# Causal attention with the scores once, query rows on partitions, and the probabilities turned by TensorE

## What is computed

```python
qb = jnp.moveaxis(q.reshape(B, nb, ATTN_BLOCK, H, Dq), 1, 0)       # Dq = 64 + 32, ATTN_BLOCK = 128
def one_block(args):
    q_blk, i = args
    s = jnp.einsum('bqhd,bkhd->bhqk', q_blk, k).astype(jnp.float32) * scale
    s = jnp.where(kpos[None, :] <= qpos[:, None], s, -jnp.inf)
    p = jax.nn.softmax(s, axis=-1).astype(v.dtype)
    return jnp.einsum('bhqk,bkhd->bqhd', p, v)                     # values are 64 wide
```

## Time and profile before

| | |
|---|---|
| runs of the kernel before | 1379.83, 1379.10, 1374.12 us, median 1379.10 |
| the profiled execution | 1374.35 us, span 1372.6 us |
| granted TensorE clock, mean | 0.993 |
| TensorE busy | 1327.3 us, 97% |
| VectorE busy | 917.8 us, 67% |
| ScalarE busy | 452.4 us, 33% |
| GpSimd busy | 492.0 us, 36% |

### The profile page before, as it was taken

How to read it: one execution, slowest core, us unless ns; L and a number is a source line. 1 busy time by engine, 2 the same in 40 slices (tenths; PEclk the granted TensorE clock), 3 DMA queues, 4 the chain that set the end, 5 groups by cost and what they waited for, 6 DMA issues and landing times.

```text
span 1372.6 us, 22898 instructions
## 1 busy us (share of the span) xinstructions
PE 1327.3 (97%) x9644; PEld 1075.2 (78%) x9644; DVE 917.8 (67%) x997; ACT 452.4 (33%) x615; POOL 492.0 (36%) x306
## 2 busy tenths in 40 slices
PE   7999999999999989988999999999999999999997
PEld 6877677777776689985678878888888888888886
DVE  4657974363654544436787789877776786669877
ACT  3144543233344333323114431222212444333330
POOL 0000122040577100100065787767664355444030
PEclk9999999999999999999999999999999999999999
DMA  5111354678348942223123235444445986656662
GB/s 221 62 47 46 123 184 154 165 178 255 116 137 279 231 126 55 50 73 138 62 107 108 85 130 177 166 157 154 141 144 202 357 285 229 198 185 194 201 200 110
DMA packets 144726, 213.77 MB, mean 156 GB/s; under 512 B 79368, under 2 KB 82064, under 8 KB 143984
## 3 DMA queue, kind: packets, MB, share of 16 engines
q1 hardware_dynamic: 144336, 211.26, 48.3%
q10 hardware_dynamic: 288, 1.05, 0.2%
HBM read 137.76 MB, written 66.39 MB: 149 GB/s over the span
## 4 chain that ended last, share of the span: by engine, by line
PE 50%; DVE 2%; POOL 1%; issue 1%; ACT 0%; DVEq 0%; POOLq 0%; ACTq 0%
PE banks L2508 22%; PE banks L2398 18%; PE banks L2314 6%; PE banks L2386 2%; POOL tile_h L3064 1%; PE banks L2359 1%; POOL tile_s L3064 0%; PE banks L2340 0%; PE banks L156 0%; DVE first_relu L2856 0%; PE banks L2325 0%; DVE wout_lo L2719 0%; DVE y_all L2739 0%; DVE y_all L2735 0%; PE banks L150 0%
## 5 line engine op out<-in xcount | busy, mean ns | idle before, releaser
L2508 PE MATMUL banks<-stage_b_hi,stage_a_hi 128*128 128x512 f32 x448 | 174.3, 389 | 0.0
L2508 PE MATMUL banks<-stage_b_lo,stage_a_hi 128*128 128x512 f32 x448 | 174.3, 389 | 0.0
L2508 PE MATMUL banks<-stage_b_hi,stage_a_lo 128*128 128x512 f32 x448 | 174.3, 389 | 0.0
L2884 DVE TENSOR_TENSOR stage_a_lo<-stage_a_raw,stage_a_hi 128x1024 fp32r<-128x1024 f32 x56 | 100.6, 1796 | 40.2 <-ACT stage_a_hi L2648 40.2
L2648 ACT ACTIVATE stage_a_hi<-stage_a_raw 128x1024 fp32r<-128x1024 f32 x56 | 59.4, 1061 | 119.6 <-DMA stage_b_raw<-in_w_ffn 99.0
L2508 PEld LDWEIGHTS banks<-stage_b_lo,stage_a_hi 128*128 128x128 f32 x448 | 84.1, 188 | 17.6
L2508 PEld LDWEIGHTS banks<-stage_b_hi,stage_a_lo 128*128 128x128 f32 x448 | 84.1, 188 | 17.5
L2508 PEld LDWEIGHTS banks<-stage_b_hi,stage_a_hi 128*128 128x128 f32 x448 | 84.1, 188 | 17.3
L428 PE MATMUL banks<-xT_hi,win_hi 128*128 128x512 f32 x288 | 90.6, 396 | 0.0
L428 PE MATMUL banks<-xT_lo,win_hi 128*128 128x512 f32 x288 | 88.8, 389 | 0.0
L428 PE MATMUL banks<-xT_hi,win_lo 128*128 128x512 f32 x288 | 88.7, 389 | 0.0
(11 more groups left out here) (424 smaller groups left out, 3585.9 us busy)
## 6 DMA issues: line engine op xcount, KB each, us to landing
stage_b_raw<-in_w_ffn SPq DMA_DIRECT2D x50, 512.0 KB, 5.0
stage_a_raw<-hid_s SPq DMA_DIRECT2D x32, 512.0 KB, 4.0
w_landed<-in_w_ffn SPq DMA_DIRECT2D x30, 512.0 KB, 4.9
hid_s<-tile_s SPq DMA_DIRECT2D x60, 256.0 KB, 4.3
stage_a_raw<-hid_h SPq DMA_DIRECT2D x24, 512.0 KB, 4.1
hid_h<-tile_h SPq DMA_DIRECT2D x42, 256.0 KB, 2.0
win_raw<-in_w_in SPq DMA_DIRECT2D x20, 512.0 KB, 3.6
x_tok<-in_x SPq DMA_DIRECT2D x8, 512.0 KB, 7.8
```

The lines of the kernel that those rows point to most:

```text
L2508: last = nc.tensor.matmul(ps[:, bank, :], s[a][:, j, tok], s[b][:, j, :], start=p == 0 and j == 0 and n == 0, stop=p == NP - 1 and j == 1 ...
L2884: V.tensor_tensor(s["a_lo"][:], s["a_raw"][:], s["a_hi"][:].bitcast(F32), ALU.subtract).then_inc(lo2, 1)
```

## The change

The one-pass scores, the turned maxima and the ones beside the values go. `scores(h, i)` (L1202) makes the three-pass scores once, 128 queries on partitions, from the last query block (i = 0) to the first, in units of up to 512 keys: 12 units in a head, over banks 0 to 3. VectorE reduces each unit and makes the bias -scale x maximum of the block; ScalarE's exponential (L1343) takes it as a pointer and also writes the sum of each row (`accum_out`). `turn_probs` (L1217) transposes the probabilities in blocks of 128x128, 36 in a head, into banks 4 and 5; ScalarE copies out the even units (L1355), VectorE the odd ones. `pv` (L1241) has the values of one head as a 64-column operand and puts the products of two pairs of query blocks into the two column halves: queries 4 to 7 are the group LATER (bank 6), 0 to 3 EARLIER (bank 7). `inverse_out` (L1251) spreads the inverse sums with eight products of the same form into the same bank. ScalarE copies both with one operation of 128x512 per group, GpSimd multiplies.

nope 3 moves to FRONT, LATE keeps key 2 (ahead of head 1) and key 3 (ahead of head 3). Head 6's output leaves by GpSimd and SyncE like the others. The first chunk of the recurrence has its V from an early load, `first_v`; the reciprocals in the chunks go. In `mix_out` `spreading` stands ahead of `early(3)`, and two `dot_step` calls stand behind the first two output steps. The memsets of constants for row 96 and the ones go.

```diff
-    LATE_TURNS = {0: ("late", None), 1: (None, 7), 2: (6, 5), 3: (4, 3), 4: (2, 1), 5: (0, None), 6: (None, "m")}
-    TAKES = [(qt, (0, 1) if qt >= TT // 2 else ((TT - 1 - qt) % 2,)) for qt in S_ORDER] + [("m", (0, 1))]
-    BANKS = dict(TAKES)
-    USES = [sum(b in banks for _, banks in TAKES) for b in range(2)]
-    FREES = [n - 1 for n in USES]
+    UNITS = [(2 * i, 2 * i + 1) if i < TT // 2 else (i + TT // 2,) for i in range(TT)]
+    NU = 12
+    LATER, EARLIER = 0, 1
+    BANK_T, BANK_Y = 4, 6
+    QUERY = lambda i: TT - 1 - i
+    blocks_of = lambda i, u: QUERY(i) + 1 if i >= TT // 2 else (4 if u == 2 * i else QUERY(i) - 3)
+    group_of = lambda i: LATER if i < TT // 2 else EARLIER
+    def landing(i, u):
...
-             ("nope", 1), ("key", 1), ("nope", 2))
+             ("nope", 1), ("key", 1), ("nope", 2), ("nope", 3))
     EARLY = 2
...
+            def scores(h, i):
...
+                rows = slice(qt * P, (qt + 1) * P)
+                for u in UNITS[i]:
+                    n = NU * h + u
+                    if n >= 4:
+                        pe.wait_ge(exp_done, n - 3)
+                    elif n == 2:
+                        left(FRONT[11])
+                    first = 4 * P if i < TT // 2 and u % 2 else 0
+                    width = blocks_of(i, u) * P
+                    diag = u == UNITS[i][-1]
+                    keys, out = slice(first, first + width), ps[:, u % 4, 0:width]
+                    for m, (qq, kk) in enumerate(((q_hi, k_hi), (q_hi, k_lo), (q_lo, k_hi))):
+                        last = mm(out, qq[z][0:96, rows], kk[z][0:96, keys], start=m == 0, stop=m == 2 and not diag)
...
+                        last = mm(out[:, width - P:width], causal_r[:], ident_r[:], start=False, stop=True)
+                    last.then_inc(s_done, 1)
...
+            def turn_probs(h, i):
+                for u in UNITS[i]:
+                    n = NU * h + u
+                    pe.wait_ge(exp_done, n + 1)
+                    if n >= 2:
+                        pe.wait_ge(evicted[u % 2], n // 2)
+                    elif n == 0:
+                        left(FRONT[9])
+                    for j in range(blocks_of(i, u)):
+                        last = nc.tensor.transpose(ps[:, BANK_T + u % 2, j * P:(j + 1) * P],
+                                                   probs[n % 3][:, j * P:(j + 1) * P], ident[:])
+                    last.then_inc(t_done, 1)
...
+            def pv(h, g, kts):
+                if kts[0] == 0:
+                    for e in range(2):
+                        pe.wait_ge(evicted[e], NU // 2 * h + (4, 6)[g])
+                    if h:
+                        pe.wait_ge(y_read[g], h)
...
+                        left(FRONT[10])
+                for kt in kts:
+                    for c in range(2):
+                        q0 = (4, 0)[g] + 2 * c
+                        if kt > q0 + 1:
+                            continue
+                        if g == LATER:
+                            src, at = ((late_t[0][:, kt, :], 4) if kt < 4 else (late_t[1][:, kt - 4, :], 4) if kt < 6
+                                       else (late_t[2][:, kt - 6, :], 6))
+                        else:
+                            src, at = (early_t[0][:, kt, :], 0) if kt < 2 else (early_t[1][:, kt - 2, :], 2)
+                        lo = max(kt, q0) * P
+                        last = mm(ps[64 * c:64 * c + 64, BANK_Y + g, lo - q0 * P:2 * P], v_all[:, kt, h, :],
+                                  src[:, lo - at * P:(q0 + 2 - at) * P], start=kt == 0, stop=kt == q0 + 1)
+                if kts[-1] == (7, 3)[g]:
+                    last.then_inc(pv_done[g], 1)
+            def inverse_out(h, g):
+                pe.wait_ge(inverse_ready[g], h + 1)
+                for j in range(2):
+                    for c in range(2):
+                        last = mm(ps[64 * c:64 * c + 64, BANK_Y + g, (2 + j) * P:(3 + j) * P],
+                                  inverse_sums[:, 2 * c + j, :], ident[:], start=True, stop=True)
+                last.then_inc(y_done[g], 1)
...
+            scores(0, 0)
+            front(FRONT[11])
+            EARLY_KTS = {0: (0,), 1: (1,), 2: (2, 3)}
+            LATE_KTS = {4: (0, 1), 5: (2, 3), 6: (4, 5), 7: (6, 7)}
...
+                for i in range(TT):
+                    late = i == TT - 1 and h + 1 in LATE
+                    if h == 0 and i == 0:
+                        turn_probs(h, i)
+                    if late:
+                        late_item(h + 1)
+                    elif i < TT - 1:
+                        scores(h, i + 1)
+                    elif h < NH - 1:
+                        scores(h + 1, 0)
+                    if h and i in EARLY_KTS:
+                        pv(h - 1, EARLIER, EARLY_KTS[i])
+                        if i == 2:
+                            inverse_out(h - 1, EARLIER)
+                    if i in LATE_KTS:
+                        pv(h, LATER, LATE_KTS[i])
+                        if i == TT - 1:
+                            inverse_out(h, LATER)
+                    if h or i:
...
+                    if late:
+                        scores(h + 1, 0)
+            pv(NH - 1, EARLIER, (0, 1, 2, 3))
+            inverse_out(NH - 1, EARLIER)
...
+                act.wait_ge(bias_ready, TT * h + i + 1)
+                qt = QUERY(i)
+                for m, u in enumerate(UNITS[i]):
+                    n = NU * h + u
+                    if n >= 3:
+                        act.wait_ge(t_done, n - 2)
+                    width = blocks_of(i, u) * P
+                    A_(probs[n % 3][:, 0:width], ps[:, u % 4, 0:width], ACT.Exp, bias=bias[:, qt:qt + 1], scale=SCALE,
+                       accum_out=sums[:, m, qt:qt + 1]).then_inc(exp_done, 1)
+            def evict(h, i):
+                for u in UNITS[i]:
+                    if u % 2:
+                        continue
+                    act.wait_ge(t_done, NU * h + u + 1)
+                    if h:
+                        act.wait_ge(pv_done[group_of(i)], h)
+                    for dst, first, n in landing(i, u):
+                        last = A_(dst, ps[:, BANK_T, first * P:(first + n) * P].rearrange("p (n q) -> p n q", n=n), ACT.Copy)
+                    last.then_inc(evicted[0], 1)
...
+                A_(k.att_q[g][:], ps[:, BANK_Y + g, :], ACT.Copy).then_inc(y_read[g], 1)
+            def sweep(h):
+                for i in range(TT):
+                    exps_of(h, i)
+                    if h == 0 and i == 0:
+                        stage_product(FRONT[11])
+                    if i:
+                        evict(h, i - 1)
+                    if h and i == 0:
+                        y_out(h - 1, LATER)
+                    if h and i == 3:
+                        y_out(h - 1, EARLIER)
...
+            def maxima(h, i):
+                qt = QUERY(i)
+                for m, u in enumerate(UNITS[i]):
+                    dve.wait_ge(s_done, NU * h + u + 1)
+                    step.mark(V.reduce_max(tops[:, m, qt:qt + 1], ps[:, u % 4, 0:blocks_of(i, u) * P], AX_X))
...
+                if len(UNITS[i]) == 2:
+                    V.tensor_scalar(bias[:, qt:qt + 1], tops[:, 0, qt:qt + 1], tops[:, 1, qt:qt + 1], -SCALE, ALU.max, ALU.mult)\
...
+            def evict(h, i):
+                for u in UNITS[i]:
...
+                    for dst, first, n in landing(i, u):
+                        last = V.tensor_copy(dst, ps[:, BANK_T + 1, first * P:(first + n) * P].rearrange("p (n q) -> p n q", n=n))
+                    last.then_inc(evicted[1], 1)
...
+            def invert(h, g):
...
+                row_sums = sums[:, 0, of]
+                if g == LATER:
+                    step.mark(V.tensor_tensor(total[:], sums[:, 0, of], sums[:, 1, of], ALU.add))
+                    step.wait()
+                    row_sums = total[:]
+                step.mark(V.reciprocal(inverse[:, of], row_sums))
+                step.wait()
+                if h or g == EARLIER:
+                    dve.wait_ge(y_done[1 - g], h + g)
+                V.tensor_copy(inverse_sums[:],
+                              inverse[:, of].rearrange("p (n o) -> p n o", o=1).to_broadcast([P, 4, HD]))\
+                    .then_inc(inverse_ready[g], 1)
...
+            rest(("key", 1))
+            rest(("nope", 2))
+            maxima(0, 0)
+            rest(("nope", 3))
...
+                if m == 1 or m and m % 4 == 0:
                     pe.wait_ge(v_in[m // 4], 16)
...
-                                  start=True, stop=True)
+                        v = hT[own[p], T_V + c, now(m)] if m else k.first_v[own[p], c, :]
+                        last = mm(ps[own[p], B_V, cols(c)], v, centre[own[p], :], start=True, stop=True)
                 last.then_inc(tr_done, 1)
...
                 gate(0, c)
-            early(3)
             for c in range(2):
                 spreading(0, c)
+            early(3)
```

395 lines of the change are left out of this document (125 added, 270 removed).

## The result

The changed kernel takes 1380.74 us (median of 20 runs, 1378.27 to 1384.58), the kernel before 1378.16 (20 runs, 1374.12 to 1380.98). The ratio is 1.0024, 95% interval 1.0015 to 1.0034: 0.24% slower. That is less than the 0.5% that the prediction took as the least that can be told, but the interval lies above 1, so the sign is clear. The forecast was 1388. The profiled execution took 1382.34, span 1380.5, so the two profiles lie 8.0 us apart where the medians lie 2.6 apart: the one of before was 3.8 quicker than its median, this one 1.6 slower. What follows is therefore read by stage. One run in all of this case lies far off, 2666.93 us in e8_early3_first; it enters no ratio.

What follows compares the result with a forecast made beforehand. TensorE, busy 97% of the span, was taken as the bound. Beginning +4.6, steady heads +8.8, irregular heads +1.0, clock +1.7 and behind the attention -4.3 gave +11.8 us: 1388, own range 1382 to 1396, wider range 1369 to 1402.

Steps and rivals of the forecast that it cites:

- (b): Rival: grouping changes cost half and row sums nothing, half the saving returns as waits: +5, 1382; chance 0.27.
- (c): Rival: changes of grouping are free in the seven groups of a head: -8, 1369; chance 0.20.
- Products and changes of grouping: TensorE in a steady head: 11.1 us removed, 11.95 added, seven grouping changes at 0.37 each: +0.85 a head.
- Waits of a steady head: TensorE waiting for ScalarE's evictions at blocks 3 (1.0) and 4 (0.8): 1.8 us, 0.5 more than before.
- Irregular heads: Heads 0 to 3, with fewer late products, -2.8; the last head, ending with EARLIER's products, +3.8: together +1.0 us.
- The clock: At the loop's thinner start, one more stretch of 3.4 us at the lower clock: +1.7 us.
- The beginning: Start of the loop's scores, late through nope 2's transfers and staging, maxima and nope 3: +4.6 us.
- The first chunk: Recurrence's start: the wait for V goes, -2.2 us, and 1.1 of the low clock behind it is taken back.
- mix_out: Spreading ahead of early(3) shortens the wait for yr_full, taken as 1.0 us; the moved dot steps cost 0.
- (d): Rival: one stretch of 3.4 us at the lower clock in each attention head: +25, 1401; chance 0.05.
- (e): Rival: the column halves of the values' products run one after another: +35, 1412; chance 0.03.

Runs made afterwards that it cites:

- e8_early3_first: e1 with early(3) ahead of the spreading again, as before the change: 1379.5 us, ratio 1.0018 to the kernel before.
- e3: Changed kernel with each of the four LATER pieces of a head cut in two, four more changes of column grouping a head: 1388.8 us, ratio 1.0091.
- e10: e6 with nope 2 and nope 3 exchanged in FRONT and block 0's maxima and exponentials ahead of nope 2's staging: 1365.6 us, ratio 0.9901.
- e6: e1 with the values' products merged into three groups a head and ScalarE's evictions ahead of the exponentials: 1364.8 us, ratio 0.9921.
- e9: e1 with ScalarE's evictions ahead of the exponentials and nothing merged: 1367.0 us, ratio 0.9924.
- e7: e1 with the recurrence's first chunk taking V from the reload again, as before the change: 1374.9 us, ratio 0.9987.
- e1: Changed kernel with the two dot steps ahead of the first output steps again, spreading still ahead of early(3): 1375.0 us, ratio 0.9982.

## Why the forecast was wrong, step by step

The direction was right and the size was not: in the profile's terms +11.8 was forecast and +8.0 came. Between the medians it is +2.6; the other 5.4 are no step of the prediction, since they lie in which executions were profiled (3.8 of them in the one of before). The rival (b), half-price changes of grouping within 6.9 us, comes nearest in time (1382, at +5), in part by luck: a change costs 0.25 of 0.37 and not half, the row sum isn't free, and no more waits came in return but fewer. A head of 19 to 20 had been named as the sign of (c), free changes; it came (19.97) with changes that aren't free, so it was no sign that tells them apart.

- **Products and changes of grouping, the step that failed most.** The term was 4.7 + 0.85 + 2.6 = 8.15 a head. From the timeline of a steady head the same seven groups take about 7.4 (corners and the wait of 0.80 taken off). The products were priced right; a change costs 0.25, not 0.37. The 0.1 that I added for a late start of what follows was already in the distance that the earlier trace rows show. With 7.4, and 3.7 for the transposes, TensorE's work in a head rises by nothing: 11.1 removed, 11.1 added. Over eight heads that is 6.8 us. The Trainium skill ("TensorEngine Tiling (Array Packing)", Key Properties) says that a change of mode drains TensorE; e3 agrees, with 0.25 to 0.34 a group.
- **Waits of a steady head.** The places and releasers were right, both ScalarE's evictions behind exponentials. Their size was 0.15 and 0.80 in place of 1.0 and 0.8. The price of an exponential isn't why: pointer and sum cost 0.09 each, the 0.19 of the forecast. ScalarE and VectorE had less to do in a head, 11.7 and 11.6 in place of 14.5 and 13, which fits a shorter chain, but what made the first wait short isn't shown. Together with the first step: a head of 19.97 in place of 21.2, -9.8 over eight.
- **Irregular heads.** From the first scores of block 1 on, heads 0 to 3 take 0.9 more than before, the last head 3.5 more. Against steady heads that is +1.5, where -2.8 and 1.7 of clock were forecast, and +3.7, where it was 3.8. The last head was right; the first four hold the clock's part, below.
- **The clock.** I added one stretch of 3.4 us; there are three more (13.7 against 3.4), worth up to 5.1 in place of 1.7. The step failed because I counted stretches and did not ask how long TensorE would go on being interrupted behind the start: waits of 3.62, 1.40 and those of the first blocks follow each other. e10, whose longest wait there is 1.56, has no such stretch; e6 and e9, with 4.05 and 3.12 at the first transposes, have one of 10.2, so the waits alone don't give its length.
- **The beginning.** +4.6 forecast, +3.15 measured, by the chain that was written down: transfers behind the turn, nope 2's staging, maxima, nope 3.
- **The first chunk.** -3.3 forecast, -2.7 in the profiles and -1.6 by e7.
- **mix_out, the other step that failed.** The spreading's move was taken at -1.0; it is worth -4 (e8). "Two dot steps behind the first output steps ...: 0, no engine waits for them" was wrong by 6 (e1): on VectorE they stand ahead of a wout_lo that TensorE waits for, 1.3, and SyncE waits for them ahead of the load of x, with loads of w_out queued behind it, 3.0; the rest went with a stretch of lower clock. Net +2.8 where I had -1.0 (-4.1 and +6.3, and 0.6 by which e8's mix_out is longer than that of before). I had followed what waits for the dot products on TensorE, and neither VectorE's own order nor SyncE's queue.
- **(d), the clock falling in every head, did not come.** The granted clock is 1.00 in the steady heads, with 36 transposes in each. The rule of the Trainium skill ("TensorE: Matmul & The Clock Gate", Part 4) that transposes don't count as busy shows nowhere as a fall here. (e), halves one after the other, did not come either, by the eight records in 1.01 us; its +35 is 11.8 and 8 x 5.55 with the 20.8 for the changes taken off, which it doesn't say.

What stays open: how much of the half clock behind the start is cost, since no run has that start without it and the rest unchanged; and what lengthens single chunks of the recurrence from run to run.
